# Inverse square roots moved from ScalarE to VectorE, and another start of the gather ring, in a two-block kernel on Trainium2

## What is computed

```python
def rms_norm(x, g, eps=EPS):
    y = xf * lax.rsqrt(jnp.mean(xf * xf, axis=-1, keepdims=True) + eps)
    return (y * g.astype(jnp.float32)).astype(x.dtype)

def layer_norm(x, g=None, b=None):
    y = (xf - mu) * lax.rsqrt(var + LN_EPS)

def block(hb):                       # 128 tokens
    ...
    u = expert_u[idx]
    act = jax.nn.gelu(jnp.einsum('thkd,td->thk', u, hb), approximate=False)
    vv = expert_v[idx]
    return jnp.einsum('thk,thkd->td', gate * act, vv)
```

## Time and the profile before

| | |
|---|---|
| runs | 2435.77, 2431.96, 2430.18 us; median 2431.96 |
| profiled execution | 2429.78 us; span 2428.0, granted PE clock 0.906 |
| busy share of the span | PE 86%, DVE 64%, ACT 50%, POOL 33% |
| moved by DMA | 729.71 MB, mean 301 GB/s |
| gathers | 467 into AR and 45 into WR, 1 MB each |

### The profile page before, as it was taken

The page is one execution under the profiler, slowest core; times in us unless marked ns, Lnnn a source line. Parts: engine busy times, 40 slices in busy tenths (PEclk is TensorE's granted clock), DMA queues, the critical chain, the costliest instruction groups (busy, mean ns, idle before and its releaser), DMA issues.

```text
span 2428.0 us, 34184 instructions
## 1 busy us (share of the span) xinstructions
PE 2081.3 (86%) x12956; PEld 1589.9 (65%) x12956; DVE 1543.4 (64%) x3428; ACT 1211.8 (50%) x2391; POOL 802.9 (33%) x684
## 2 busy tenths in 40 slices
PE   6989998897797886666669999776998999989998
PEld 4445576786555655555567788645887757858863
DVE  5565665688865677788566686566666544955422
ACT  1123331466657667666676567767776740111110
POOL 2000000365643333455544895333332310800000
PEclk9999888998898998666679999987999999999999
DMA  4322245788899999999999999999999975353431
GB/s 169 121 96 69 73 146 206 285 325 306 352 354 395 415 418 415 420 421 419 417 418 415 414 362 417 415 418 414 409 413 412 412 297 193 113 189 107 172 139 69
DMA packets 162133, 729.71 MB, mean 301 GB/s; under 512 B 10161, under 2 KB 13361, under 8 KB 95921
## 3 DMA queue, kind: packets, MB, share of 16 engines
q0 software_dynamic: 73728, 536.90, 54.7%
q1 hardware_dynamic: 88240, 190.62, 21.5%
HBM read 725.38 MB, written 2.10 MB: 300 GB/s over the span
## 4 chain that ended last, share of the span: by engine, by line
PE 45%; DMA 25%; DVE 15%; ACT 9%; issue 4%; POOL 2%; SPq 0%; DVEq 0%; ACTq 0%; POOLq 0%
DMA AR<-in_uv,C 19%; PE PA L923 12%; PE PD L1510 7%; PE PA L1442 4%; PE PD L923 4%; ACT AR L2026 3%; PE PA L1455 3%; DVE AR L2944 2%; DMA WR<-in_w_up 2%; DMA WR<-in_w_down 2%; DVE AR L2888 2%; PE PD L1087 2%; PE PA L1584 2%; PE PD L1584 2%; POOL AR L3179 1%
## 5 line engine op out<-in xcount | busy, mean ns | idle before, releaser
L2888 DVE CUSTOM_DVE_ANT_0 AR<-AR,HN 128x1024 f32<-128x1024 f32 x467 | 587.9, 1264 | 344.1 <-issue 180.8
L3179 POOL DMA_INDIRECT AR<-in_uv,C x467 | 558.7, 1196 | 711.7 <-PE PD L1510 669.3
L1510 PE MATMUL PD<-C,AR 128*128 128x128 f32 x3736 | 594.0, 313 | 221.1 <-ACT AR L2026 219.9
L1510 PEld LDWEIGHTS PD<-C,AR 128*128 128x128 f32 x3736 | 504.7, 162 | 351.9 <-ACT AR L2026 299.4
L2026 ACT ACTIVATE AR<-AR,SC 128x1024 f32<-128x1024 f32 x467 | 536.6, 1149 | 15.2
L2022 ACT ACTIVATE SC<-SC 128x1 f32<-128x1 f32 x512 | 103.7, 203 | 368.8 <-DVE SC L2888 367.7
L3179 POOL DMA_INDIRECT WR<-in_uv,C x45 | 52.4, 1164 | 464.1 <-DVE C L2621 394.7
L923 PE MATMUL PA<-HT,WR 128*128 128x256 f32 (+1 forms) x608 | 185.2, 465 | 0.9 <-ACT AR L2045 0.9
L1442 PE MATMUL PA<-HT,WR 128*128 128x256 f32 x704 | 168.7, 386 | 12.1 <-DMA WR<-in_w_up 12.1
L923 PE MATMUL PA<-AR,WR 128*128 128x256 f32 (+1 forms) x896 | 170.4, 353 | 0.7 <-ACT AR L1803 0.7
L923 PEld LDWEIGHTS PA<-AR,WR 128*128 128x128 f32 x896 | 152.6, 193 | 17.7 <-ACT AR L1803 1.1
(11 more groups left out here) (495 smaller groups left out, 3088.5 us busy)
## 6 DMA issues: line engine op xcount, KB each, us to landing
WR<-in_w_up SPq DMA_DIRECT2D x22, 2048.0 KB, 18.0
WR<-in_w_in SPq DMA_DIRECT2D x18, 2048.0 KB, 8.5
WR<-in_w_ada SPq DMA_DIRECT2D x12, 2048.0 KB, 8.3
WR<-in_w_down SPq DMA_DIRECT2D x9, 2048.0 KB, 9.4
WR<-in_w_pq SPq DMA_DIRECT2D x8, 2048.0 KB, 16.4
WR<-in_w_o SPq DMA_DIRECT2D x4, 2048.0 KB, 18.4
WR<-in_w_out SPq DMA_DIRECT2D x4, 2048.0 KB, 18.9
AR<-in_uv,C POOLq DMA_INDIRECT x467, 14.6
```

Source lines behind the costliest of these rows:

```text
L1510: ins = nc.tensor.matmul(acc[i // 4][:, P * (i % 4):P * (i % 4) + P], uv_row(j, D + P * i, D + P * i + P), ident, start=(k == 0 and i % 4 ...
L2888: ttr(uv_row(j, 0, D), uv_row(j, 0, D), HN[:, t, :], 1.0, 0.0, ALU.mult, ALU.add, DOT[:, j:j + 1]).then_inc(s["dots"], 1)
L3179: nc.gpsimd.indirect_dma_start(uv_row(ring_slot(turn), 0, 2 * D), None, uv, bass.IndirectOffsetOnAxis(ap=IDX[:, t % 2, i:i + 1], axis=0),) ...
```

## The change

It has two parts. First, 35 of the 38 inverse roots no longer go to ACT. DVE shifts the variance's bits right by one and subtracts them from a constant (a guess), and refines it in three Newton steps of three instructions: eleven linked instructions where there were a copy, a wait, a reciprocal and three. ACT has 35 roots fewer, and of 95 table loads in its program 60 remain.

Second, the ring has its five slots 0, 8, 9, 10 and 11 from turn 0. Two chunks of `w_pq` take other buffers: columns 1536 and up (queries 12 to 15) come into `WR` 0 behind query 11 instead of into `WR` 1 behind query 7. The queries 12 to 15 stand behind rows 7, 8 and 10 instead of 2, 3 and 4, one score group behind row 13 instead of 7, the first tile's matrices behind rows 14, 16 and 18. POOL waits for query 7 at turn 3 instead of for query 15 at turn 8, and the memset with its wait (for query 15 now) stands at turn 12 instead of 5.

```diff
-PHASES = ((0, (8, 9, 0)), (6, (8, 9, 10, 11, 0)), (52, (9, 3, 5, 6, 0, 4, 8)), (66, (7, 3, 5, 6, 0, 4)),
+PHASES = ((0, (0, 8, 9, 10, 11)), (52, (9, 3, 5, 6, 0, 4, 8)), (66, (7, 3, 5, 6, 0, 4)),
...
-MATRIX_AT = {1: (11, 13, 15), 2: (33, 35, 36), 3: (39, 41, 42)}
+MATRIX_AT = {1: (14, 16, 18), 2: (33, 35, 36), 3: (39, 41, 42)}
...
-FIRST_QUERY_AT = {0: (8, 9), 1: (10, 11), 2: (12, 13), 3: (14,), 4: (15,)}
-FIRST_SCORE_AT = {4: 3, 7: 4}
+FIRST_QUERY_AT = {0: (8, 9), 1: (10, 11), 7: (12,), 8: (13, 14), 10: (15,)}
+FIRST_SCORE_AT = {4: 3, 13: 4}
+CLEAR_AT = 12
...
-        col_chunk(w_pq, 512, 512, "a", FIRST_A[("query", 7)])
-        col_chunk(w_pq, 1024, 512, "a", FIRST_A[("f", 3)])
-        col_chunk(w_pq, 1536, 512, "uv", FREED[10] - 1)
-        SLOTS += [1, 2, 0, 3, 1, 0, 1]
+        col_chunk(w_pq, 512, 512, "uv", FREED[10] - 1)
+        col_chunk(w_pq, 1024, 512, "a", FIRST_A[("query", 11)])
+        col_chunk(w_pq, 1536, 512, "a", FIRST_A[("f", 3)])
+        SLOTS += [1, 2, 0, 3, 1, 0, 0]
...
-            roots(st_a[:, 0:4])
...
+            def inverse_root(dst, v_, w_):
+
+                bits = dst.bitcast(U32)
+                link(ts(bits, v_.bitcast(U32), 1, None, ALU.logical_shift_right))
+                link(ts(bits, bits, -1.0, 1597463007.0, ALU.mult, ALU.add))
+                for _ in range(3):
+                    link(tt(w_, dst, dst, ALU.mult))
+                    link(stt(w_, w_, -0.5, v_, ALU.mult, ALU.mult))
+                    link(stt(dst, w_, 1.5, dst, ALU.add, ALU.mult))
+
             def rstd(dst, scale, eps):
...
-                tell(nc.vector.tensor_copy(dst, v_), "var")
-                dve.wait_ge(s["rstd"], n["var"])
-                link(nc.vector.reciprocal(r_, dst))
-
-                link(tt(v_, v_, r_, ALU.mult))
-                link(stt(v_, v_, -0.5, r_, ALU.mult, ALU.mult))
-                link(stt(dst, v_, 1.5, r_, ALU.add, ALU.mult))
+                inverse_root(dst, v_, w_)
...
-                if row == 5:
+                if row == CLEAR_AT:
                     own_done()
-                    pool.wait_ge(s["a_full"], FIRST_A[("query", 11)] + 1)
+                    pool.wait_ge(s["a_full"], FIRST_A[("query", 15)] + 1)
...
-                    if turn == 8:
-                        pool.wait_ge(s["a_full"], FIRST_A[("query", 15)] + 1)
+                    if turn == 3:
+                        pool.wait_ge(s["a_full"], FIRST_A[("query", 7)] + 1)
```

More of the change, by code:

```diff
@@ L1693, in _ @@
             for t in range(NT):
-                roots(st_a[:, 16:32])
                 raw(t)
@@ L1931, in early_functions @@
                     tell(A(GBA, GBA, ACT.Sigmoid), "sigg")
-                for t in range(2):
-                    if r in (NORMED_AT[t] + 1, NORMED_AT[t] + 5):
-                        roots(ffv(t))
                 for J in range(NF // 2):
@@ L1994, in evictions_behind @@
                     first_scores(FIRST_SCORE_AT[row])
[L1996 to L1999, removed]
             for t in range(NT):
@@ L2006, in _ @@
                         sum_back(t - 1)
-                    if t > 0 and k == NORM_AT[t][1] - 1:
-                        roots(ffv(t - 1))
                     if t == 2 and k == TURN_AT[t] + 2:
@@ L2016, in _ @@
                                 part_exp(t_, i)
-                    if row in ROOTS_AT:
-                        roots(ROOTS_AT[row])
                     if part_begin(t, k) is not None:
@@ L2037, in _ @@
             sum_back(NT - 1)
-            roots(ffv(NT - 1))
             for t in range(2):
                 tell(nc.scalar.copy(downed(t, 0), take()), "a_free")
-            for t in range(2):
-                roots(ffv(t))
             act.wait_ge(s["d_full"], FIRST_D["acc"] + 8)
@@ L2340, in attention_variance @@
                 link(ts(sinb[:, a:b], cosb[:, a:b], 1.0 / 64, EPS, ALU.mult, ALU.add))
-                tell(nc.vector.tensor_copy(cosb[:, a:b], sinb[:, a:b]), "var")
             def attention_rstd(a, b):
[L2345 to L2350, removed]
+                inverse_root(cosb[:, a:b], sinb[:, a:b], sinb[:, 32 + a:32 + b])
             def attention_scale(t):
@@ L2418, in output_scaled @@
                 y, st, w_, r_ = HN[:, t, 512:1024], st_a[:, 16:24], cosb[:, 32:40], cosb[:, 40:48]
[L2419 to L2423, removed]
+                inverse_root(st, w_, r_)
                 ins = tt(h3(y), h3(y), st.unsqueeze(2).broadcast_to([P, H, 64]), ALU.mult)
@@ L2642, in mixed @@
                     link(ts(w_, v_, 1.0 / D, EPS, ALU.mult, ALU.add))
-                    tell(nc.vector.tensor_copy(v_, w_), "var")
                 elif step == 2:
[L2645 to L2649, removed]
+                    inverse_root(v_, w_, r_)
                 else:
@@ L2679, in layer_step @@
                     link(ts(root[:, 16:17], v_, 1.0, LN_EPS, ALU.mult, ALU.add))
-                    tell(nc.vector.tensor_copy(v_, root[:, 16:17]), "var")
                 elif step == 1:
[L2682 to L2687, removed]
+                    inverse_root(v_, root[:, 16:17], root[:, 0:1])
                 else:
@@ L2722, in variance @@
                 link(ts(root[:, 16:17], st[:, 13:14], 1.0, LN_EPS, ALU.mult, ALU.add))
[L2723 to L2732, removed]
             def mixed_rows(step, t):
@@ L2744, in mixed_rows @@
                 elif step == 3:
-                    inverse_root(v_)
+                    inverse_root(v_, root[:, 16:17], root[:, 0:1])
                     link(stt(xt, xt, st[:, 12:13], R2A[:, 2048:3072], ALU.subtract, ALU.mult))
```

11 lines of the change are left out of this document (1 added, 10 removed).

## The result

The changed kernel takes 2462.30 us, median of 4 runs (2458.88 to 2472.24), against 2433.86 of the kernel before (4 runs). The ratio is 1.0124, with a 95% interval from 1.0098 to 1.0149. It is slower, as forecast, but by 28 us instead of 17, and above the range. The profiled execution has a span of 2470.4 us, 42.4 more than that of before; it is the slowest of the four, so what its trace shows of the loss is more than the median's.

A forecast was written before the change was run, and what follows sets the result against it. No one engine limits all: gathers pace 620 to 690 and 797 to 1952 us, PE 436 to 494 and the end. 2429.8 + 11.3 + 6.3 + 2.5 - 0.9 = 2449.0 us; range 2437 to 2458.

The forecast's parts named there:

- The roots' instructions: Prologue and last stage: twelve roots on the critical path, seven and five, each 0.94 us longer on DVE, +11.3 us.
- the clock behind the pause at turn 12: Row 12: PE's granted clock falls to 0.50 after its pause, as at row 0, +2.5 us (0 if it holds).
- the forecast's own range: Range of the summed forecast: 2442 (half the roots covered, clock held) to 2454 us (covers gone); chance 0.57.
- Turn 12: Row 12: POOL's wait for query 15, memset and mask delay the gather; +6.3 us, plus 2.5 for the clock.
- The 1.3 us of Exp's table: Ahead of row 0: Exp's table load of 1.28 us leaves the chain, -1.3 us, already in the next step's times.
- Roots among the rows: Row roots at L2420 and L2646: six more instructions each but no wait for ACT; -0.9 us at L2420, 0 at L2646.
- the pause is given back: Rival, rows from 494 to 797 us: delayed rows run faster and make turn 12 good, 2439 or 2433; chance 0.16.
- Late weights: Rival, query 12: the last `w_pq` chunk comes late and PE waits 11 us, 2454 to 2460; chance 0.17.
- ACT was the bound: Rival, rows from 494 to 1952 us: 35 fewer table loads give back up to 44.8 us, 2404; chance 0.10.

The follow-up runs named there:

- the pair above: Two kernels with row roots, five-slot ring, late memset and filled PE pauses, differing by the 19 `rstd` roots (DVE or ACT): 2440.48 and 2428.05 us.
- the ring alone: The change's ring, tables and memset put into the kernel before, roots left on ScalarE: 2443.67 us, ratio 1.0037.
- the kernel with PE kept busy: The changed kernel with useless identity transposes for PE in four pauses (67 us, 152 us, ahead of row 0 and row 12): 2450.94 us.
- the run of the row roots: The kernel before, ring unchanged, with only roots among the rows or split into steps on VectorE; the 19 `rstd` roots stay on ScalarE: 2432.30 us, ratio 1.0002.
- the roots alone: The changed kernel with ring, tables, chunks, waits and memset put back as before, keeping its roots on VectorE: 2454.02 us, ratio 1.0079.
- the delay alone: The kernel before with useless small VectorE instructions ahead of two prologue norms (5 and 18), nothing else changed: 2442.44 us, ratio 1.0043.
- the late memset: The changed kernel with the memset and its wait for query 15 at turn 26 instead of 12: 2451.09 us.
- the repaired change: The changed kernel, all 35 roots on VectorE, with the memset at turn 26 and PE kept busy in three pauses: 2440.48 us, ratio 1.0033.
- the last kernel: The kernel before plus row roots on VectorE, five-slot ring, memset at turn 26 and transposes in three PE pauses: 2428.05 us, ratio 0.9981.

## Why the forecast was too low

**The roots' instructions: right.** 12 roots at 0.94 us were to cost 11.3 us; the pair above has 12.4, and the steps in the trace are 0.91 to 0.95 at the twelve places named. An estimate by the formula of the Trainium skill ("VectorE: DVE Perf Modes", the section on the TRN2 errata) was 6.4: instructions are 0.16 to 0.17 busy, as it says, but follow each other at 0.20 to 0.21.

**What the roots do to PE's clock: missing.** This is the step that failed: "12 x 0.94 = +11.3 us" stood for all that the roots cost on the path. The same prediction priced the clock behind the pause at turn 12, and did not ask which pauses of PE in the prologue the roots lengthen. Two of them it lengthens from 2.17 to 3.10 and from 1.56 to 5.25 us. In the profiled execution the clock made 22.2 us out of 7.5; in the median, keeping PE busy there and ahead of row 0 is worth 2451.09 - 2440.48 = 10.6 us (11.0 by the distances from before), of which about 2.5 belong to row 0. So some 8 us were missing, and in the profiled execution nearly twice that. The measured time lies above the forecast's own range as well; that range, 2442 to 2454, comes out of its terms as 2441 to 2456.

**Turn 12: right in its mechanism, near in its sum partly by luck.** 6.3 + 2.5 = 8.8 us were forecast. The dots have 10.3 from row 0 to row 102, the ring alone costs 11.5 (2443.67 - 2432.19), and moving the memset gives 9.5 to 11.2 back. POOL's wait, the memset and the mask are as named, but the two terms missed in opposite directions. Up to the start of row 12's transposes the trace has 9.2 instead of 6.3. The 1.3 us of Exp's table did not come, since row 0's dot waited for its gather as long as before (6.7 us from issue to dot, 6.9 before); and row 12's dot took 2.62 us instead of 1.23, in a chain of 4.4 instead of 3.0 from dot to scaling:

```profile
520.93 2.62 DVE L2835 CUSTOM_DVE_ANT_0 WR<-WR,HN 128x1024 f32<-128x1024 f32 x1 [16.55 <-DMA WR<-in_uv,C]
```

No run tells why; it is as long (2.63 to 2.82) in the three other kernels that wait at turn 12. The clock did fall behind the pause (row 12's transposes took 1.97 us), but of the 2.5 us only some 0.9 are left by row 102: from row 12's dot to that one the kernel with PE kept busy, where the clock held, gains 0.9 on before, and the changed one 0.1.

**Roots among the rows: nothing against it.** -0.9 was forecast; with those roots alone it is 0, within 3 to 4 us either way, which cannot tell the two apart.

**The rivals.** That the pause is given back fell: the 10 us stand unchanged from row 12 to row 102. Late weights fell: PE came to query 12 without a wait. That ACT was the bound fell with the run of the row roots, which takes the long waits for ACT away, with 26 table loads of 1.28 us, and gains nothing. No rival was the one that happened.

**What stays open.** What makes the clock fall behind a given pause: a longer one makes it likelier, and each kernel has one profile only. Whether the fall at 242 to 263 us, the largest, belongs to the change. It stands in three profiles of those that lengthen the pauses (the changed kernel, the roots alone, the delay alone), in none of the others, and not in the one with the late memset, whose pauses were as long; the pause just ahead of it is 1.4 us with it and without. That it needs the earlier falls was not tried. The last stage, behind row 511's dot, grew by 8.5 us, of which five roots are 4.6. It grew by 7.2 with the roots alone and by 3.2 with the ring alone, which changes nothing there, and no experiment told why.

## What to carry to other kernels

An instruction added to a chain that TensorE waits for costs its own time and, where it makes TensorE's pause longer, it can cost what the lower clock takes from the work behind it: price both, at every such pause and not only at the largest. Moving work off a lightly used engine is no gain where that engine answered in 0.27 us; count the linked instructions on the side that receives it. And a wait put in an in-order queue of gathers stops all gathers behind it: move the wait to where its condition is long true, which here was one number.

## What the runs showed of the hardware

The granted clock is not the same from execution to execution (a mean of 0.902 to 0.910 over 23 runs of the kernel before), and a short pause can go either way: 2.17 us with the clock kept in the kernel before, 2.17 us with the clock at 0.52 behind it in another. In the kernel with the delay alone, whose times spread over 22.5 us (2433.44 to 2455.97), the slower half has the lower clock. Whether filling the pauses narrows the spread is not shown: it is 9.0 us (2436.70 to 2445.71) for the repaired change, but 13.6 us for the last kernel, whose pauses are filled too, and 21.8 us (2422.60 to 2444.35) over those 23 runs of the kernel before. At 245 to 255 us the clock of the changed kernel stayed at 0.50 for the whole 10 us although PE was busy for 10.00 of them.
